# A fused two-layer float32 block: value products of attention in groups, and the order of work around the attention stage

## The reference, cut to what matters

```python
x = first_block(...)          # FFN, attention with two branches, output projection, FFN, gate
return second_block(x, ...)   # HGRN recurrence, convolutions, FFN (not touched)

# inside first_block, 512 positions, 16 heads of 64 in two families of 8 (NSA and FOX)
o_a = gg[..., 0:1] * o_c + gg[..., 1:2] * o_s + gg[..., 2:3] * o_w  # compressed, selected, window
logits = einsum('bhqd,bhsd->bhqs', qq, k) * scale + cq - c          # FOX
p = softmax(where(kpos <= tpos, logits, NEG));  o_b = einsum('bhqs,bhsd->bhqd', p, v)
mixed = concatenate([rmsnorm(merge_heads(o_a), out_norm_nsa),
                     rmsnorm(merge_heads(o_b), out_norm_fox)], axis=-1)
h = h + mixed @ w_out
```

## Time and profile before

| what | value |
|---|---|
| median of 3 runs | 2124.58 us (2124.04 to 2130.04) |
| the profiled execution | 2124.41 us, its span 2122.5 us |
| PE busy, whole span | 2083.7 us (98%) |
| DVE, ACT, GpSimd busy | 856.3, 718.9, 910.5 us (40, 34, 43%) |
| first scores of attention | 548.14 us |
| first product of the output projection | 698.95 us |
| behind it, 708 to 997 us | the chain of waits lies on PE almost without a break |

### The profile page before, as it was taken

One profiled execution on the slowest core, in us unless ns is written; L12 is line 12 of the kernel. 1 busy time (PEld: TensorE's weight loads), 2 busy tenths in 40 slices (PEclk: granted clock), 3 DMA queues, 4 the chain that ended last, 5 costly groups with the idle time before them and its releaser, 6 DMA issues.

```text
span 2122.5 us, 38056 instructions
## 1 busy us (share of the span) xinstructions
PE 2083.7 (98%) x15692; PEld 1795.3 (85%) x15692; DVE 856.3 (40%) x1251; ACT 718.9 (34%) x1083; POOL 910.5 (43%) x690
## 2 busy tenths in 40 slices
PE   8999999999999999999999999999999999999998
PEld 7888888877777788887888998999999898998887
DVE  4222300587766432222107527833221446556302
ACT  4222221445678432223214532321122332322213
POOL 4444444445321444434444544434443044445442
PEclk9999999999999999999999999999999999999999
DMA  5223222432100232332222222122322122322221
GB/s 181 86 92 99 99 92 86 144 107 69 33 3 3 70 99 79 99 99 98 87 93 87 92 87 74 62 76 84 99 80 85 35 80 79 99 92 87 98 99 60
DMA packets 152344, 179.03 MB, mean 84 GB/s; under 512 B 7093, under 2 KB 142750, under 8 KB 152238
## 3 DMA queue, kind: packets, MB, share of 16 engines
q1 hardware_dynamic: 152075, 177.43, 25.8%
q10 hardware_dynamic: 163, 0.04, 0.0%
HBM read 175.37 MB, written 2.10 MB: 84 GB/s over the span
## 4 chain that ended last, share of the span: by engine, by line
PE 73%; issue 13%; POOL 8%; DVE 4%; ACT 1%; DMA 1%; SPq 0%; POOLq 0%; DVEq 0%; ACTq 0%
PE ps L1955 48%; PE ps L2096 11%; POOL wlo L689 8%; PE ps L2593 2%; PE ps L2391 2%; PE ps L2361 1%; PE ps L2374 1%; DVE tmp L1329 1%; PE ps L2494 1%; PE ps L2356 1%; DMA raw<-in_ffn_wu 1%; PE ps L2192 1%; PE ps L2400 0%; PE ps L2444 0%; PE ps L2223 0%
## 5 line engine op out<-in xcount | busy, mean ns | idle before, releaser
L689 POOL TENSOR_TENSOR wlo<-raw,whi 128x512 fp32r<-128x512 f32 x634 | 850.0, 1373 | 1077.7 <-ACT whi L778 1073.0
L1955 PE MATMUL ps<-xh,whi 128*128 128x258 f32 (+2 forms) x2400 | 686.9, 333 | 3.0 <-issue 2.0
L1955 PE MATMUL ps<-xh,wlo 128*128 128x258 f32 (+2 forms) x2400 | 681.7, 331 | 0.0
L1955 PE MATMUL ps<-xl,whi 128*128 128x258 f32 (+2 forms) x2400 | 680.0, 330 | 0.0
L778 ACT ACTIVATE whi<-raw 128x2048 fp32r<-128x2048 f32 (+1 forms) x158 | 301.3, 1907 | 767.8 <-PE ps L1955 477.1
L1955 PEld LDWEIGHTS ps<-xh,whi 128*128 128x128 f32 x2400 | 406.5, 189 | 53.9 <-issue 4.6
L1955 PEld LDWEIGHTS ps<-xh,wlo 128*128 128x128 f32 x2400 | 405.4, 188 | 47.5 <-issue 4.0
L1955 PEld LDWEIGHTS ps<-xl,whi 128*128 128x128 f32 x2400 | 405.2, 189 | 43.6
L2096 PE MATMUL ps<-act_l,whi 128*128 (+1 forms) x528 | 208.6, 395 | 0.0
L2096 PE MATMUL ps<-act_h,wlo 128*128 (+1 forms) x528 | 208.6, 395 | 0.0
L2096 PE MATMUL ps<-act_h,whi 128*128 (+1 forms) x528 | 208.6, 395 | 0.0
(11 more groups left out here) (352 smaller groups left out, 2348.7 us busy)
## 6 DMA issues: line engine op xcount, KB each, us to landing
raw<-in_w_in SPq DMA_DIRECT2D x47, 1024.0 KB, 5.1
raw<-in_ffn_wg SPq DMA_DIRECT2D x22, 1024.0 KB, 5.4
raw<-in_ffn_wu SPq DMA_DIRECT2D x22, 1024.0 KB, 5.3
raw<-in_ffn_wd SPq DMA_DIRECT2D x22, 1024.0 KB, 4.9
raw<-in_w_up SPq DMA_DIRECT2D x22, 1024.0 KB, 5.1
raw<-in_w_down SPq DMA_DIRECT2D x11, 1024.0 KB, 4.9
raw<-in_w_out SPq DMA_DIRECT2D x8, 1024.0 KB, 5.0
raw<-in_ple_w_gate SPq DMA_DIRECT2D x4, 1024.0 KB, 5.0
```

Source lines behind the costliest of these rows:

```text
L689: last = nc.gpsimd.tensor_tensor(wlo[:, slot, d], raw[:, slot, d], whi[:, slot, d].bitcast(F32), ALU.subtract)
L1955: last = mm(ps[:, j * banks + b, 0:n], w[:, k, e * P:(e + 1) * P], x[:, k, c0:c0 + n], start=(k == 0 and q == 0), stop=(k == KD - 1 and q ...
```

## The change

Value products are held back and done by groups. A group is the three branches of one query block; the first group of a head has the compressed step too. The products of group g follow the transposes in the iteration that starts group g+2 (`VALUES_AT`), and the outputs of its steps come one in each of the next iterations (`out_at`). A group's outputs share one bank, at different columns. `probT` has six slots in place of three. GpSimd's splits of queries wait for scores in place of outputs.

In the prologue DVE does `head_norm(13)` and three of the four `stage_fox_c` later, inside the loop (`LAST_NORM`: steps 18, 19, 24, 25 and 31), and `stage_fox_k(0)` after the first maximum; ACT copies `fox_values(2)` and `values(1)` ahead of the compressed values, and the FOX queries after the first exponential.

Behind the loop the output norm's statistics are taken by query block: blocks 0, 3 and 1 first, block 2 last; DVE squares and sums the last three heads of blocks 1 and 2 (`late_sums`), ACT makes six of the diagonal tiles. Six tiles n (0 to 5) are turned ahead of the output projection, into six banks, and two between its products.

```diff
-LAG_T, LAG_V, LAG_O = 2, 4, 5
+LAG_T = 2
+GROUPS = NH * TT
+SLOTS_T = 6
+def group(s):
+    n, r = divmod(s, PER_HEAD)
+    return TT * n + max(r - 1, 0) // len(BRANCHES)
+FIRST = [s for s in range(NS) if s == 0 or group(s) != group(s - 1)] + [NS, NS + 2]
+VALUES_AT = {FIRST[g + 2]: g for g in range(GROUPS)}
+def out_at(s):
+    return [q for q in range(NS) if values_at(q) + max(1, 4 + q - FIRST[group(q) + 1] if group(q) < GROUPS - 1 else 4 + q - NS) == s]
+TURNED_BANK = (0, 1, 2, 3, 4, 5, 0, 1)
+LAST_NORM = [18, 19, 24, 25, 31]
...
-                pool.wait_ge(o_done, PER_HEAD * (n - 1) + 2)
+                pool.wait_ge(score_done, PER_HEAD * (n - 1) + 5)
...
+            fox_values(2)
+            values(1)
             act.wait_ge(vcmp_zero, 1)
...
-            values(1)
-            fox_values(2)
-            act.wait_ge(tiles_done, used_count(W_OUT1 - 1))
-            stage_fox_q(0)
             fox_values(3)
...
+                    if s == 0:
+                        act.wait_ge(tiles_done, used_count(W_OUT1 - 1))
+                        stage_fox_q(0)
...
-                    if q >= 3:
-                        act.wait_ge(pv_done, q - 2)
-                    nc.scalar.activation(probT[:, q % 3, 0:i + 1, :],
+                    if q >= SLOTS_T:
+                        act.wait_ge(pv_done, q - SLOTS_T + 1)
+                    nc.scalar.activation(probT[:, q % SLOTS_T, 0:i + 1, :],
...
-            for n in range(2 * TT - 4, 2 * TT):
-                last_square(n)
...
+            def diagonals(b):
+                for half in range(2):
+                    nc.scalar.activation(diag[:, half, BLOCKS[b], :], ident[:], ACT.Copy,
+                                         scale=rstd[:, 2 * b + half:2 * b + half + 1]).then_inc(diag_made, 1)
+            out_root(0, 6, 1)
+            act.wait_ge(orstd, 1)
+            diagonals(0)
+            diagonals(1)
+            out_root(6, 8, 2)
+            diagonals(2)
...
-            head_norm(13)
...
+            def late_sums(b, done):
+                i = BLOCKS[b]
+                heads = otok[:, i, :].rearrange("p (e c) -> p e c", e=2)[:, :, (NH - 3) * HD:NH * HD]
+                sq = prob[:, 2, 0:6 * HD].rearrange("p (e c) -> p e c", e=2)
+                dve.wait_ge(o_done, done)
+                nc.vector.tensor_tensor(sq, heads, heads, ALU.mult).then_inc(late_sq, 1)
+                nc.vector.tensor_reduce(rstd[:, 8 + 2 * b:10 + 2 * b], sq, AX_X, ALU.add).then_inc(late_sq, 1)
...
+                    if q == NS - 4:
+                        late_sums(2, NS - 3)
+                        dve.wait_ge(osq_done, 12)
+                        sums_added(0, 6)
...
+            nc.vector.reciprocal(rstd[:, 0:6], std[:, 0:6]).then_inc(orstd, 1)
+            late_sums(3, NS)
+            sums_added(6, 8)
...
-                if s >= LAG_V:
-                    q = s - LAG_V
-                    pe.wait_ge(ptev_done, q + 1)
-                    if q >= 2:
-                        pe.wait_ge(o_done, q - 1)
+                if s in VALUES_AT:
+                    g = VALUES_AT[s]
+                    if g >= 2:
+                        pe.wait_ge(o_done, FIRST[g - 1])
+                    for q in range(FIRST[g], min(FIRST[g + 1], NS)):
+                        ob, oc = 6 + g % 2, out_column(q)
+                        pe.wait_ge(ptev_done, q + 1)
...
-            for n in range(4):
-                turned_out(n)
+            for b in range(3):
+                for n in range(6):
+                    pe.wait_ge(diag_made, 2 * b + n // 4 + 1)
+                    turned_out(n, b)
+            for n in range(6):
+                pe.wait_ge(diag_last, n // 4 + 1)
+                turned_out(n, 3).then_inc(otr, 1)
...
-                if k < 4:
-                    turned_out(4 + k)
+                if k < 2:
+                    for b in range(TT):
+                        last = turned_out(6 + k, b)
+                    last.then_inc(otr, 1)
```

More of the change, by code:

```diff
@@ L440, in build @@
         diag_made = sem("diag_made")
+        diag_last = sem("diag_last")
+        late_sq = sem("late_sq")
         otr = sem("otr")
@@ L1103, in _ @@
                 gain = col("out_norm_nsa", n) if n < 4 else col("out_norm_fox", n - 4)
-                nc.scalar.activation(mixh[:, n, M:T], ps[:, 4 + n % 4, :], ACT.Copy, scale=gain).then_inc(xh_ready, 1)
+                nc.scalar.activation(mixh[:, n, M:T], ps[:, TURNED_BANK[n], :], ACT.Copy, scale=gain).then_inc(xh_ready, 1)
                 if n == 3:
@@ L1559, in _ @@
             dve.wait_ge(fl_v, 8)
[L1560 to L1561 removed]
+            stage_fox_c(0)
             dve.wait_ge(gc_ready, TT)
@@ L1606, in _ @@
                                             ALU.add).then_inc(csum_done, 1)
-                if s >= LAG_O:
-                    q = s - LAG_O
+                if 1 <= s // PER_HEAD < NH - 1 and s % PER_HEAD == 9:
+                    if s // PER_HEAD + 1 == NH - 2:
+                        dve.wait_ge(unorm, 14)
+                    stage_fox_k(s // PER_HEAD + 1)
+                for q in out_at(s):
                     n, i, b = STEPS[q]
+                    ob, oc = 6 + group(q) % 2, out_column(q)
                     if b == CMP:
@@ L1621, in _ @@
                         weigh(stat, c, c + 3, c, gsig[:, i, 3 * n:3 * n + 2])
-                    dve.wait_ge(pv_done, q + 1)
+                    dve.wait_ge(pv_done, FIRST[group(q) + 1])
                     c0 = (S if b == FOX else 0) + HD * n
@@ L1645, in _ @@
                 dve.wait_ge(xh_ready, 2 * KD + n + 1)
-                nc.vector.scalar_tensor_tensor(mixl[:, n, M:T], ps[:, 4 + n % 4, :], gain, mixh[:, n, M:T].bitcast(F32),
+                nc.vector.scalar_tensor_tensor(mixl[:, n, M:T], ps[:, TURNED_BANK[n], :], gain, mixh[:, n, M:T].bitcast(F32),
                                                ALU.mult, ALU.subtract).then_inc(xl_ready, 1)
@@ L2323, in _ @@
             fox_values(3)
-            for s in range(NS + LAG_V):
+            for s in range(FIRST[-1] + 1):
                 if s < NS:
@@ L2395, in turned_out @@
-            def turned_out(n):
-                if n >= 4:
-                    pe.wait_ge(xl_ready, 2 * KD + n - 3)
-                for i in range(TT):
-                    pe.wait_ge(diag_made, n // 4 * TT + i + 1)
-                    last = mm(ps[:, 4 + n % 4, i * P:(i + 1) * P], otok[:, i, n * P:(n + 1) * P], diag[:, n // 4, i, :],
-                              start=True, stop=True)
-                last.then_inc(otr, 1)
-            def out_products(n, k):
-                return products(n % 4, n % 2, (W_OUT1 + n // 2) % 2, (mixh, mixl), WHOLE, 1, k)
@@ new lines, in turned_out @@
+            def turned_out(n, b):
+                i = BLOCKS[b]
+                return mm(ps[:, TURNED_BANK[n], i * P:(i + 1) * P], otok[:, i, n * P:(n + 1) * P], diag[:, n // 4, i, :],
+                          start=True, stop=True)
+            def out_products(n, k):
+                return products(out_bank(n), n % 2, (W_OUT1 + n // 2) % 2, (mixh, mixl), WHOLE, 1, k)
+            for b in range(3):
+                for n in range(6):
+                    pe.wait_ge(diag_made, 2 * b + n // 4 + 1)
+                    turned_out(n, b)
```

115 lines of the change are left out of this document (70 added, 45 removed).

## The result

The changed kernel takes 2110.39 us (median of 4 runs, 2108.78 to 2112.38) against 2125.26 us (4 runs, 2124.04 to 2130.04) for the kernel before. The ratio is 0.9928, with a 95% interval of 0.9916 to 0.9940. The profiled execution took 2110.16 us, with a span of 2108.0 us against 2122.5. The forecast was 2108.0 us, 16.6 less than before; measured are 14.9 less by the medians and 14.5 by the spans.

The account below looks back on a forecast made before the run. PE was taken to set the pace of the attention stage. The terms -14.5 - 2.9 + 2.0 + 0.7 + 0.5 - 0.1 - 2.3 gave -16.6 us, so 2108.0 us; own range 2104 to 2112, 8 in 10 within 2102 to 2116.5.

Parts of the forecast that it names:

- The mechanism and its price: On PE, changing between whole array and 32-column products costs 0.14 + 0.09 us a pair; 64 pairs go: -14.5 us.
- Longer lead: In the attention loop, the output stall that lengthens every second head goes: -2.9 us.
- Hand-over: In the loop, scores, exponentials and transposes run late around grouped value products: 0.3 us a head, +2.0, bounds 0 to 1.0 a head.
- a sign of being wrong: PE waiting for exponentials over half a microsecond a head, in iterations without value products, would point to rival A or D.
- rival A: ACT and DVE partly pace the loop; hand-over costs 1.0 us a head: -10.6 us in all, 2114 us; chance 0.22.
- The norm in the loop: head_norm(13)'s reciprocal parts in head 1 and product in head 2 lengthen DVE's head: +0.7 us, between 0.3 and 2.
- The squares' head: In the head taking the early squares, ACT's 14.87 us stays while PE's falls to 14.7: +0.5 us, between 0 and 1.
- Prologue: Ahead of the loop, DVE's work shrinks by 5 us but FOX scores start at 551.9: -0.1 us, between -1 and +1.
- Tail: Behind the last output: 6.8 to 9.5 us to the projection, two turned groups fewer later: -2.3 us, between -3.6 and -0.9.
- C: The fixed part belongs to each step's value products, not the array shape: only -2 us, 2122 us; chance 0.03.
- D: ACT idles through each group's value products, heads 17.5 us instead of 17.0: slower, 2128 to 2129 us; chance 0.04.
- B: The lead is fully enough, so hand-over, norm and squares cost nothing in the loop: -22 us, 2102 us; chance 0.12.

Follow-up runs that it names:

- the whole-array kernel: The kernel before, with each key block's value product done as one whole-array product instead of four 32-column ones: 2126.98 us in one run.
- The kernel with the added products between the steps: The changed kernel plus 64 short bf16 whole-array products, one ahead of the second and third step's value products in every group: 2126.06 us.
- the pair of kernels above: The changed kernel plus 64 short whole-array products, either between the steps of each group (2126.06 us) or two together ahead of each group (2115.59 us).
- the one with the filler at the stage's start: The changed kernel plus 26 unread transposes of the identity on PE behind its first transpose, where it waits for the FOX key's split: 2108.24 us.
- the norm's move: The changed kernel with head_norm(13) and all four fills back in DVE's prologue, behind negsel and the clearing of vcmp: 2108.74 us.
- 20/12 of them: The changed kernel with the norm back in the prologue, 20 unread transposes at the stage's start and 12 behind the last value product: 2104.61 us.
- the fillers alone: The changed kernel plus 26 unread transposes at the stage's start and 16 behind the last value product, norm left in the loop: 2112.92 us.

## Why the prediction was right

*The mechanism and its price: right, and shown.* The fixed 0.14 + 0.09 us was read from the trace of before, and stands unchanged in the trace after, once for each group. What reaches the stage is less, as the hand-over takes some back: 0.15 to 0.17 us a pair by the experiments, 0.18 to 0.21 in plain heads, and 16.54 - 15.07 = 1.47 for 8 pairs, 0.18, between the two kernels. The Trainium skill (TensorEngine Tiling (Array Packing), Key Properties) says that changing the tiling mode drains the engine. The traces agree: the fixed time stands where the shape changes, and is missing between two steps of one shape and in the whole-array kernel. Its price here is 0.23 us for both directions on PE.

*Longer lead: right.* No wait for an output lengthens every second head any more (1.2 us of such waits are left in seven heads, in the second of the PEld rows above). The kernel with the added products between the steps has the old number of changes and the new lead, and its plain heads are even, 16.75 to 16.78 us, where those of before alternate between 16.5 to 16.7 and 17.3 to 17.6.

*Hand-over: right in time, near its limit in kind.* The forecast for a plain head was 16.54 - 1.81 + 0.3 = 15.03 us, and it is 15.07. The hand-over is seen in the 10.4 us ahead of the transposes. I had named waits for exponentials of over half a microsecond a head as a sign of being wrong. By PE's own rows a plain head has none; by its weight load the plain heads have 0.6 us, and the heads with the norm's product and the squares 1.9 and 1.5. So that sign is just passed by one reading, and rival A was nearer than the time of a plain head shows.

*The norm in the loop: mis-sized.* Forecast +0.7 us, measured 1.8, inside its bounds of 0.3 to 2. The error lies in the value chosen between them: I compared DVE's busy time with PE's head, and that was not what counts. Each piece stands ahead of maxima that PE is soon waiting for. One of the four reciprocals, which I had put all into head 1, comes in head 2 like the product, and the product is longer than its nearest row made it:

```profile
580.49 0.94 DVE L1632 RECIPROCAL tmp<-tmp 128x128 f32<-128x128 f32 x1
...
586.45 1.28 POOL L770 TENSOR_TENSOR qs<-uT,qs 64x512 fp32r<-64x512 f32 x1 [6.68 <-ACT qs L993]
586.72 1.56 DVE L1635 SCALAR_TENSOR_TENSOR uT<-uT,cols,tmp 128x512 f32<-128x512 f32 x1
...
590.35 0.66 PE L2464 MATMUL ps<-ident,prob 128*128 128x128 f32 x4 [0.66 <-ACT prob L1110]
```

The same instruction in the prologue of before, with GpSimd (POOL) idle:

```profile
533.57 0.75 DVE L1463 SCALAR_TENSOR_TENSOR uT<-uT,cols,tmp 128x512 f32<-128x512 f32 x1
```

From 480 us to the end of the prologue of before it takes 0.75 us each of the three times that no instruction of GpSimd overlaps it, and 0.91 to 1.87 us the five times that one does.

*The squares' head:* forecast +0.5, measured 16.01 - 15.07 = 0.9, within its bounds of 0 to 1. Together with the norm that is 1.5 us of the 2.2 by which the loop fell short. The rest, 0.7, is in the stretch from the last head's mask to the last output, 20.52 us before and 20.74 after. I had given that head its share of the gain. Up to the last step's mask it has one, 15.11 us against 14.15. Behind that mask it loses 1.2: 5.41 us became 6.59. The value products of the last two groups now stand behind all scores, and PE waits for a copy in between:

```profile
675.68 0.92 PE L2484 MATMUL ps<-vtok,probT 128*32 128x64 f32 x48 [0.63 <-ACT probT L1133]
```

What shorter groups at the end would give was not tested.

*Prologue: right.* DVE's split and the FOX scores stand where the forecast had them, 551.9 against 551.25:

```profile
546.90 0.29 DVE L1661 TENSOR_REDUCE cstat<-ps 128x4 f32<-128x128 f32 x1 [10.88 <-PE ps L2445]
548.73 2.31 DVE L1676 TENSOR_TENSOR whi<-uT,whi 64x512 fp32r<-64x512 f32 x2
551.25 0.26 PE L2448 MATMUL ps<-causal,ident_b 128*128 128x128 bf16 x1 [2.94 <-DVE whi L1676]
```

The first row shows what I had not priced: with the norm gone, DVE stands idle for 10.88 us. The norm went into the loop, where it costs 1.8 us, while the prologue had room in which it costs nothing.

*Tail: mis-sized.* Forecast -2.3, between -3.6 and -0.9, and measured -1.6. PE's wait fell from 3.71 us to 1.82, less than the 2.5 expected, but the low clock came all the same (7.25 us instead of 5.62). The first product came 8.62 us behind the last output, inside the 6.8 to 9.5 named, but for a wrong reason: 1.0 us of that sum stood for sums ahead of the last output, which lie outside this stretch and cost nothing. Without it the range is 5.8 to 8.5. The sum also counted 19 tiles, where PE turns all 24 ahead of the first product; even at the full clock that product comes at 7.00 us. The two turned groups fewer behind it are the whole gain.

*The rivals.* C and D fell: the pair of kernels above excludes C, and no head comes near D's 17.5 us but the first (17.72), which runs partly at the low clock. B fell too, since PE does wait for exponentials. A was right in kind in two heads, those with 14.16 us on DVE and 14.62 us on ACT, where PE itself waits 1.0 and 0.8 us for exponentials; in plain heads both engines are busy for 12.6 us of 15.07, and PE is busy for 15.02. The rule of the Trainium skill that I set beside A (TensorEngine Tiling (Array Packing), PSUM Bottleneck) holds here only where other work was put on those engines.

*The sum.* Loop -12.0, tail -1.6 and start -0.7 are -14.3, and the spans differ by 14.5, against -16.6 forecast: the loop is 2.2 short, the tail 0.7, and the start gave 0.6 more.

## What to carry to other kernels

A change between whole-array and 32-column products cost about a fifth of a microsecond for both directions here. Put products of one shape together, or do without the narrow ones where their runs are short: for one or two key blocks the whole array was cheaper (0.24 and 0.39 us against 0.34 and 0.46 with the fixed parts), for three and four it was not. Work that an engine can do in a stretch in which it is idle anyway is not made cheaper by spreading it over a loop in which others wait for that engine: price it by what is queued behind it, not by the engine's busy share. When a stage gets shorter, compare the later stretches too, since a few microseconds can come back where nothing was changed; look there for pauses of PE that no releaser explains, and for instruction packets beside them.

## What the runs showed of the hardware that I had not expected

- With the same wait of 1.82 us ahead of the turned tiles, the granted clock fell in the changed kernel (7.25 us for the tiles) and did not in the one with the filler at the stage's start, 125 us earlier (5.62 us). What decides between them no run here shows.
- Transposes that nobody reads can pay for themselves in the stage: the norm's move and 20/12 of them took it from 140.1 to 135.4 us, of which the norm's move alone is 1.4. Whether the kernel keeps that depends on what lies behind: with the fillers alone it took 2112.92 us, the changed kernel on the same chip 2111.93.
- fp32 products over the whole array with 64 columns cost 0.21 us a key block, against 0.11 for four column strips, and had no fixed part at either end.
- DVE's 128x512 SCALAR_TENSOR_TENSOR took 0.75 us alone and up to 1.88 us beside an instruction of GpSimd.
- In long runs of small products PE stands for up to 2 us at a time with no releaser in the trace, 1.7 to 7.1 us in 81 to 87, and differs between two profiles of one kernel. Each of the 42 pauses over 0.4 us ended 2.15 to 2.71 us after an instruction packet of 16 KB had started.
